# The order of flips, scores, values and the two projections in the banded attention chunks

## The reference

```python
hn = rmsnorm(x, norm_g[l]); proj = hn @ w_in[l]
u, g_main, q_mem, g_mem = jnp.split(proj, [D_MAIN, 2*D_MAIN, 2*D_MAIN+D_MEMW], axis=-1)
# layer 1:
q = rope(u.reshape(B, T, N_HEADS, HEAD_DIM), pos)
y = sink_attend(q, k_att, v_att, mask, sinks[l - N_A])   # 128 queries see 256 keys, banded
om = mem_attend(q_mem, mem_k[l], mem_v[l])
z = jnp.concatenate([y * silu(g_main), om * silu(g_mem)], axis=-1)
x = x + z @ w_out[l]
```

```python
s = where(mask, q k^T * HEAD_DIM**-0.5, NEG); m = maximum(max(s), sink)
p = exp(s - m); p = p / (sum(p) + exp(sink - m)); y = p v
```

## Time and profile before

| | |
|---|---|
| median of 3 runs | 2206.07 us (2206.01 to 2207.53) |
| the profiled execution | 2206.03 us, its span 2203.7 us |
| TensorE busy (matmuls) | 2136.0 us, 97% of the span |
| VectorE busy | 1178.0 us, 53% |
| ScalarE busy | 922.8 us, 42% |
| GpSimd busy | 86.3 us, 4% |
| mean granted TensorE clock | 0.985 |

### The profile page before, as it was taken

The page is one execution under the profiler, slowest core; times in us unless marked ns, Lnnn a source line. Parts: engine busy times, 40 slices in busy tenths (PEclk is TensorE's granted clock), DMA queues, the critical chain, the costliest instruction groups (busy, mean ns, idle before and its releaser), DMA issues.

```text
span 2203.7 us, 28279 instructions
## 1 busy us (share of the span) xinstructions
PE 2136.0 (97%) x11389; PEld 1708.6 (78%) x11389; DVE 1178.0 (53%) x2004; ACT 922.8 (42%) x1988; POOL 86.3 (4%) x54
## 2 busy tenths in 40 slices
PE   7999999999999899999999999999999997989998
PEld 6878887777777687887788887888788886767886
DVE  4854446777677822223534445777767778412222
ACT  4533335777777522223433334344444345212111
POOL 0000000000001300000300000000000005000000
PEclk9999999999999999999999999999999999979999
DMA  8111111111112465242111112222122224456331
GB/s 340 65 40 38 41 37 43 45 46 47 42 45 96 138 215 163 90 139 98 42 34 41 36 41 65 66 76 66 49 77 66 75 70 147 122 169 195 99 118 54
DMA packets 115203, 191.53 MB, mean 87 GB/s; under 512 B 13325, under 2 KB 69957, under 8 KB 110073
## 3 DMA queue, kind: packets, MB, share of 16 engines
q1 hardware_dynamic: 115073, 189.73, 26.1%
HBM read 141.28 MB, written 48.48 MB: 86 GB/s over the span
## 4 chain that ended last, share of the span: by engine, by line
PE 87%; DVE 6%; ACT 3%; DMA 2%; SPq 1%; issue 1%; DVEq 0%; ACTq 0%
PE bank L578 47%; PE bank L1864 22%; PE bank L1094 3%; PE bank L1105 2%; PE bank L681 2%; PE bank L420 2%; DMA sm_cs<-in_rope 1%; PE bank L852 1%; PE bank L1078 1%; PE bank L668 1%; PE bank L658 1%; PE bank L597 1%; PE bank L671 1%; PE bank L1852 1%; DVE in_x L307 1%
## 5 line engine op out<-in xcount | busy, mean ns | idle before, releaser
L578 PE MATMUL bank<-x_hi,w_hi 128*128 128x512 f32 x1600 | 639.6, 400 | 1.6 <-DVE w_lo L564 1.6
L578 PE MATMUL bank<-x_hi,w_lo 128*128 128x512 f32 x1600 | 626.0, 391 | 0.0
L578 PE MATMUL bank<-x_lo,w_hi 128*128 128x512 f32 x1600 | 625.2, 391 | 0.0
L578 PEld LDWEIGHTS bank<-x_hi,w_hi 128*128 128x128 f32 x1600 | 301.5, 188 | 112.2 <-issue 50.6
L578 PEld LDWEIGHTS bank<-x_hi,w_lo 128*128 128x128 f32 x1600 | 301.3, 188 | 65.0
L578 PEld LDWEIGHTS bank<-x_lo,w_hi 128*128 128x128 f32 x1600 | 301.9, 189 | 60.4 <-issue 0.4
L1864 PE MATMUL bank<-wo_hi,z_hi 128*128 128x512 f32 x768 | 303.8, 396 | 2.8 <-DVE z_lo L1695 2.8
L1864 PE MATMUL bank<-wo_hi,z_lo 128*128 128x512 f32 x768 | 300.6, 391 | 0.0
L1864 PE MATMUL bank<-wo_lo,z_hi 128*128 128x512 f32 x768 | 300.5, 391 | 0.0
L1864 PEld LDWEIGHTS bank<-wo_hi,z_hi 128*128 128x128 f32 x768 | 145.3, 189 | 36.4 <-DVE z_lo L1695 4.1
L1864 PEld LDWEIGHTS bank<-wo_hi,z_lo 128*128 128x128 f32 x768 | 145.0, 189 | 30.7
(11 more groups left out here) (312 smaller groups left out, 2769.7 us busy)
## 6 DMA issues: line engine op xcount, KB each, us to landing
w_raw<-in_w_items SPq DMA_DIRECT2D x25, 1024.0 KB, 4.9
z_scratch<-it_gz SPq DMA_DIRECT2D x96, 256.0 KB, 2.4
z_raw<-z_scratch SPq DMA_DIRECT2D x32, 768.0 KB, 5.6
it_cs<-in_rope SPq DMA_DIRECT2D x32, 512.0 KB, 4.2
wo_raw<-in_w_out SPq DMA_DIRECT2D x6, 2048.0 KB, 9.6
mk_w<-in_w_mem_kv SPq DMA_DIRECT2D x8, 1024.0 KB, 11.7
in_x<-in_x_T SPq DMA_DIRECT2D x4, 2048.0 KB, 17.0
z_x<-in_x_prompt SPq DMA_DIRECT2D x16, 512.0 KB, 4.3
```

What stands on the lines that cost most here:

```text
L578: last = nc.tensor.matmul(ps, s_, r_, start=(k == 0 and q == 0), stop=(k == KT - 1 and q == 2))
```

## The change

On TensorE the gate projection of a round moves ahead of flips and scores, so that flips of q-2, scores of q-1 and values of q-2 stand in a row behind both projections. On ScalarE the gate copies move ahead of current block and exponentials; in round 0 the copies of the last memory chunk's flips come ahead of the gate copies. VectorE, GpSimd and SyncE are unchanged; no instruction is added or removed.

```diff
@@ swa_pe
                 project(pe, "main", *ipc(q)[:2], 0, q % 4)
             if q == 0:
                 mem_flip(pe, *MEM[-1])
+            if q < NQ:
+                project(pe, "main", *ipc(q)[:2], 1, q % 4)
             if q >= 2:
                 swa_flip(pe, q - 2)
             if 1 <= q <= NQ:
                 swa_scores(pe, q - 1)
-            if q < NQ:
-                project(pe, "main", *ipc(q)[:2], 1, q % 4)
-            else:
+            if q >= NQ:
                 tail(pe, q - NQ)
             if q == 0:
                 mem_values(pe, *MEM[-1])
@@ swa_act
                 if q >= 1:
                     act.wait_ge(S["q_ready"], B["q_ready"] + q)
                 evac_branch(act, "main", *ipc(q), qraw[:, :], SWA_SCALE)
+                if q == 0:
+                    mem_flip_act(act, *MEM[-1])
+                evac_gate(act, "main", *ipc(q))
+                if q == 0:
+                    act.wait_ge(S["o_done"], B["o_done"] + G)
             if 1 <= q <= NQ:
                 swa_current(act, q - 1)
                 ahead["weights_act"](act, q)
                 swa_exp(act, q - 1)
             ahead["tiles_act"](act, q)
-            if q < NQ:
-                evac_gate(act, "main", *ipc(q))
-            if q == 0:
-                mem_flip_act(act, *MEM[-1])
-                act.wait_ge(S["o_done"], B["o_done"] + G)
             if q % 4 in (0, 1) and q < NQ - 4:
```

## The result

| | before | changed |
|---|---|---|
| median | 2206.8 us (2206.01 to 2210.33, 4 runs) | 2226.6 us (2224.52 to 2228.43, 4 runs) |
| span of the profiled execution | 2203.7 us | 2222.2 us |

The ratio is 1.0089, with a 95% interval of 1.0074 to 1.0104: slower by 0.9%. Forecast were 2223.2 us within 2213 to 2238.

What follows compares the result with a forecast made beforehand. TensorE's own work was taken to bound the steady rounds. Rounds +15.7, pipeline end +5.45 and round 0 -4.0 gave +17.2 on 2206.03 us: 2223.2 us, range 2213 to 2238.

Steps and rivals of the forecast that it cites:

- The wait that it opens: In each round the values wait on TensorE for VectorE's masks, starting at +3.61 us: 0.71 hole plus 0.06, together 0.77.
- a net of 0.58: Loss per round, 0.77 less 0.19 us, paid in 27 rounds: +15.7 us.
- What the row gives back: On TensorE projection follows projection and the values' switch falls into the hole: 0.19 us less per round.
- Nothing else is late: In the rounds VectorE's 0.26 us margin before the masks grows, ScalarE's moved gate copies cost nothing, flips don't wait.
- The end of the pipeline, +5.45: One more gate projection before the flips of 27; the 56.3 us behind them stay, last wait about 11.4: +5.45 us.
- the bound of +1.7: At the pipeline's end, 1.7 us added if the longer idle time costs one more stretch at half clock.
- Round 0, -4.0: In round 0 the values' 1.67 us wait, 0.6 in their matmuls and 1.7 of half clock go: -4.0 us.
- The clock: In the rounds the 0.7 us hole drops no TensorE clock in the sum, though flips and hole make 1.68.
- the rival's price: Clock drops in the rounds cost 1.7 us each: 2238.5 us in one round of three, 2269 in all; chance 0.12.
- The rival without a wait: In the rounds the masks fit beside the scores, so no wait: sum -3.7 us, 2202.4 us; chance 0.05.

Runs made afterwards that it cites:

- five products: Changed kernel with a fifth VectorE product of the same size, into a spare tile, before the values may start, from chunk 1 on: 2243.25 us.
- three products: Changed kernel with the last of the four mask products left out from chunk 1 on: 2205.88 us, ratio 0.9988.
- round 0 alone: Kernel before, with ScalarE's copies of the last memory chunk's flips ahead of its gate copies in round 0: 2205.51 us, ratio 0.9987.
- the control with three products: Kernel before with the last of the four mask products left out from chunk 1 on: 2205.65 us, ratio 0.9986.
- ScalarE's half alone: Kernel before with TensorE in the old order and ScalarE in the changed kernel's order: 2317.22 us.
- the three runs with holes of 2.0 to 2.6 us: Changed kernel with scores ahead of flips, 2309.64 us; changed kernel with ScalarE's old order, 2338.0 us; kernel before with ScalarE's new order, 2317.22 us.

## Why the prediction was right, point by point

The direction, the time and the mechanism held; the sum of +17.2 stands against +18.5 of span and +19.8 of the medians. Its terms were off by up to 2.2 us each, in both directions: the rounds gave 2.2 us less than forecast, the stretch behind the flips of 27 gave 2.0 more and the time behind the rounds 1.8 more. That the sum came so close is in part luck.

- *The wait that it opens.* Shown. The values start at +3.61 us, the number of the prediction, and three, four and five products move the round by 0.6 each. Mis-sized was the price of the hole, 0.77. The values start 0.71 us behind the +2.90 at which the next kind could start, as forecast (the profile calls 0.65 of that idle, from the end of the scores' last matmul at +2.96), but the 0.06 us for a first load in the open don't exist: the values take 1.97 us in both kernels. The round is 3.61 + 1.90 + 5.57 + 5.45 = 16.53. The prediction also multiplied a net of 0.58 where its own round, 16.59 less 16.05, gives 0.54. **27 x 0.50 = +13.5, not +15.7.**
- *What the row gives back.* I took 0.19 us. With three products the round is 0.12 under the old one although the values still start 0.12 late, at +3.02 instead of +2.90. So the switches are worth some 0.24 us, and 0.21 by the round of the changed kernel (0.71 less 0.50), a little more than I took. The change buys them with a start of the values that is 0.71 us later, three times as much.
- *Nothing else is late.* Held: no flips waited for the division in the rounds between, and VectorE idled before every group of masks; where the idle time had been 0.26 us it is 0.76 to 0.80, the margin that was to grow by what the round grows. The ScalarE part costs nothing only together with the other: alone, or left out, it costs over 100 us.
- *The end of the pipeline, +5.45.* The projection more before the flips of 0 is shown as 5.43, and the last wait came to 11.41 us, forecast near 11.4. But the 56.3 us behind the flips of 27, which I kept fixed, became 58.24: **+2.0 that stands in no term;** the bound of +1.7 there was for a stretch at half clock. The output weights' high parts (L1661 on ScalarE) start 3.93 us behind the flips of 27 instead of 5.05, without the wait for their load that they had before, and GpSimd's low parts (L1666) follow them. Before, these started behind VectorE's last rotation step (L1188), which took 0.69 us:

```profile
1821.83 3.90 ACT L1661 ACTIVATE wo_hi<-wo_raw 128x1024 fp32r<-128x1024 f32 x4 [1.01 <-DMA wo_raw<-in_w_out]
1822.36 0.69 DVE L1188 TENSOR_TENSOR it_qf<-it_qraw,it_qf 128x512 f32<-128x512 f32 x1
1822.97 9.56 POOL L1666 TENSOR_TENSOR wo_lo<-wo_raw,wo_hi 128x1024 fp32r<-128x1024 f32 x4 [742.80 <-ACT wo_hi L1661]
```

  In the changed kernel they start ahead of it, and it takes 2.78 us:

```profile
1835.61 3.89 ACT L1661 ACTIVATE wo_hi<-wo_raw 128x1024 fp32r<-128x1024 f32 x4
1836.73 10.32 POOL L1666 TENSOR_TENSOR wo_lo<-wo_raw,wo_hi 128x1024 fp32r<-128x1024 f32 x4 [756.94 <-ACT wo_hi L1661]
1837.26 2.78 DVE L1188 TENSOR_TENSOR it_qf<-it_qraw,it_qf 128x512 f32<-128x512 f32 x1
```

  GpSimd's four products last to 1847.05 and span that step and the maximum's first steps behind it, of which the scale L1195 and the two copies L1202 take over 2 us each in both kernels. So one step more is long, by 2.1 us, and the flips of 28 come 22.62 us behind those of 27 instead of 20.92. That the earlier start is the cause is read from the traces, no run isolates it; and the stretch from the flips of 27 to those of 28 is not steady from kernel to kernel in the rounds' old order either (20.92 us before, 18.85 with round 0 alone, 17.39 with three products).
- *Round 0, -4.0.* Measured -3.62, and 0.50 clock there is gone. The term was 0.4 too large.
- *Left out:* +1.8 behind the flips of 31. The time from there to the end is 309.73 us in the profiled execution before, but 311.56 in the control with three products and 311.3 with round 0 alone, both in the old order, and 309.87 with five products in the new order. So this is not of the change but differs from execution to execution. Why stays open: the time at half clock in that stretch, 28 us before and 34 in the changed kernel, does not order the runs (27 us of it stand beside 311.14 with ScalarE's half alone).
- *The clock.* 1.00 through all rounds, as in the sum. The Trainium skill, TensorE: Matmul & The Clock Gate (Part 4: PE-mode transpose), says that transposes don't count as busy in the way of other matmuls; with them and the hole of 1.25 us, 2.2 us in a round with the scores between, nothing dropped here, and no run tells transposes and idle time apart. In the three runs with holes of 2.0 to 2.6 us in most rounds the clock did drop, in 14 to 18 of the 27 rounds and by 1.6 us each, so the rival's price was right, and the hole of the change did not set it off. The length of a hole alone doesn't settle it. The prediction set 1.67 us in round 0, with a drop, against 0.84 without one, but the kernel before has the same wait in layer 0 too, 1.66 us, and there the granted clock (behind the count in the second row) stays at 1.00:

```profile
341.08 0.50 PE L668 MATMUL bank<-it_P_hi,it_v_hi 128*128 128x512 f32 x1 [1.66 <-ACT it_P_hi L722]
341.00:347.00 6.00, 5.92 (x25) 1.00 0.06 24
```

The rival without a wait is borne out by the run with three products, whose masks fit almost: it came to 2.5 us under the old order, near the 3.7 of the rival's sum.

## What to carry to other kernels

Count for each producer and consumer how long the other engine needs in between, here 2.5 us of masks from the end of the flips, and put at least that much independent work of the bound engine there; a switch saved is worth 0.1 us here, a hole costs all its length, and one of 2.0 to 2.6 us in most rounds cost another 1.6 us of clock in half to two thirds of the rounds. When a step moves in a software pipeline, count the steps ahead of the first and behind the last consumer: what fills at the start is not given back if the end waits on another chain. And look for what else the change touched: the one gain here, in round 0, could be had alone.

## What was not expected of the hardware

Sixteen matmuls with 64 output partitions each take 1.97 us when the two halves of the output alternate and 3.33 us when each half's eight come in a row, with the same operands and counts. The loads and matmuls themselves have the same length in both (137 and 273 ns in the middle); they overlap less. The profile counts each matmul twice, hence x32: alternating, two of these start 7 ns apart and the next two 109 ns behind them, in a row of one half a single one starts every 109 ns. The Trainium skill, TensorE: Matmul & The Clock Gate (Part 3: Packing small matmuls — row/col tiling), says that loads overlap running matmuls only for different row groups; here the rows are the same and only the columns alternate, and it was 1.4 us faster. The same section does give a gain for small matmuls packed by columns, and these rows agree with that.

Some VectorE operations beside GpSimd's products on SBUF take about 2 us more: a scale of 128x2 (L1195) that takes 0.17 us took 2.12, a sum of two tiles of 128x512 (L1188) of 0.69 took 2.78, while the copies out of a PSUM bank between them (L1203) kept their 0.59. The Trainium skill, GPSIMD Engine Reference (1. Specifications), has the two engines share their SBUF interfaces, with contention for VectorE instructions that read two SBUF inputs, as the sum does, or run in a 2-port mode; the size is of these traces.
